# MLP loops written out, buffers released by the job count, a fifth block on TensorE, late sums moved

## The reference

```python
def first_block(x, c, w_ada, b_ada, w_in, ...):
    mod = jax.nn.silu(c) @ w_ada[l] + b_ada[l]
    shift1, scale1, gate1, shift2, scale2, gate2 = jnp.split(mod, 6, axis=-1)
    u = _layer_norm(x) * (1.0 + scale1[:, None, :]) + shift1[:, None, :]
    m = _token_mixer(u, w_in[l], ...)          # 4 retention heads, 4 GLA heads
    x = _layer_norm(DEEPNORM_ALPHA * x + gate1[:, None, :] * m, ln1_w[l], ln1_b[l])
    u2 = _layer_norm(x) * (1.0 + scale2[:, None, :]) + shift2[:, None, :]
    f = jnp.square(jax.nn.relu(u2 @ w_ff1[l])) @ w_ff2[l]
    x = _layer_norm(DEEPNORM_ALPHA * x + gate2[:, None, :] * f, ln2_w[l], ln2_b[l])

# retention, per head: chunk states by a recurrence
def step(R, U_i):
    return chunk_decay * R + U_i, R

def squared_relu_mlp(x, w1, w2):
    hdn = jnp.square(jax.nn.relu(jnp.einsum('bld,df->blf', x, w1)))
    return jnp.einsum('blf,fd->bld', hdn, w2)
```

## Time and profile before

| | us |
|---|---|
| median of 3 runs | 2861.61 |
| lowest, highest | 2859.59, 2868.67 |
| the profiled execution | 2858.77 |
| its span in the profile | 2857.0 |
| granted TensorE clock, mean over the span | 0.971 |
| TensorE busy | 2662.9 |
| VectorE, ScalarE, GpSimd busy | 1446.2, 948.0, 692.7 |

### The profile page before, as it was taken

The page is one execution under the profiler, slowest core; times in us unless marked ns, Lnnn a source line. Parts: engine busy times, 40 slices in busy tenths (PEclk is TensorE's granted clock), DMA queues, the critical chain, the costliest instruction groups (busy, mean ns, idle before and its releaser), DMA issues.

```text
span 2857.0 us, 34193 instructions
## 1 busy us (share of the span) xinstructions
PE 2662.9 (93%) x13332; PEld 1367.2 (48%) x13332; DVE 1446.2 (51%) x2304; ACT 948.0 (33%) x1120; POOL 692.7 (24%) x355
## 2 busy tenths in 40 slices
PE   7999989888999999999988899788999999999998
PEld 3677666433444444444464444344544444444443
DVE  6266444567444445576575749654336622222225
ACT  3323315025223322324254353253325232222231
POOL 1211123012212212311542231136113521221222
PEclk9999999998999999999989999999999999999999
DMA  7311131202111111221021230110011111110111
GB/s 303 115 53 60 49 119 38 95 30 89 36 54 59 44 44 59 74 89 45 31 89 59 74 116 29 45 59 30 29 34 42 59 59 31 59 60 30 59 45 59
DMA packets 55583, 182.34 MB, mean 64 GB/s; under 512 B 3952, under 2 KB 4368, under 8 KB 48016
## 3 DMA queue, kind: packets, MB, share of 16 engines
q1 hardware_dynamic: 47136, 138.89, 14.2%
q10 hardware_dynamic: 8304, 41.46, 4.0%
HBM read 170.90 MB, written 9.45 MB: 63 GB/s over the span
## 4 chain that ended last, share of the span: by engine, by line
PE 72%; DVE 10%; issue 4%; ACT 4%; DVEq 3%; POOLq 3%; PEld 1%; POOL 1%; DMA 1%; ACTq 0%; PEldq 0%; SPq 0%
PE PS L680 21%; PE PS L681 21%; PE PS L682 21%; POOLq L611 1%; POOLq L609 1%; DVE XT L2077 1%; PE PS L722 1%; PE PS L1425 1%; POOL WB L555 1%; PE PS L1398 1%; DVEq L2076 1%; ACT WS L1493 1%; PE PS L971 1%; ACT WB L1491 1%; DMA Hf<-in_w_ada 1%
## 5 line engine op out<-in xcount | busy, mean ns | idle before, releaser
L555 POOL TENSOR_TENSOR WB<-WS,WB 128x512 f16<-128x512 f32 (+1 forms) x264 | 495.1, 1907 | 1898.8 <-ACT WS L1493 1898.4
L680 PE MATMUL PS<-XT,WB 128*128 128x512 f16 x1568 | 599.1, 382 | 31.7 <-issue 15.5
L681 PE MATMUL PS<-XT,WB 128*128 128x512 f16 x1568 | 598.6, 382 | 0.0
L682 PE MATMUL PS<-XT,WB 128*128 128x512 f16 x1568 | 598.1, 381 | 0.0
L680 PE MATMUL PS<-WB,Hf 128*128 128x512 f16 x1440 | 550.8, 382 | 27.2 <-issue 6.9
L681 PE MATMUL PS<-WB,Hf 128*128 128x512 f16 x1440 | 550.2, 382 | 0.0
L682 PE MATMUL PS<-WB,Hf 128*128 128x512 f16 x1440 | 549.5, 382 | 0.0
L2075 DVE CAST Hf<-S 128x512 f16<-128x512 f32 x172 | 139.8, 813 | 497.7 <-ACT S L1735 411.1
L1491 ACT ACTIVATE WB<-WS 128x2048 f16<-128x2048 f32 (+3 forms) x118 | 212.4, 1800 | 513.7 <-PEq L689 476.8
L2435 DVE SCALAR_TENSOR_TENSOR R<-PS,R 128x512 f32<-128x512 f32 x208 | 143.0, 691 | 264.9 <-PE PS L682 257.9
L680 PEld LDWEIGHTS PS<-XT,WB 128*128 128x128 f16 x1568 | 154.3, 98 | 225.5 <-issue 29.5
(11 more groups left out here) (377 smaller groups left out, 2749.8 us busy)
## 6 DMA issues: line engine op xcount, KB each, us to landing
WS<-in_w_ff SPq DMA_DIRECT2D x32, 1024.0 KB, 5.1
WS<-in_mlp_w SPq DMA_DIRECT2D x32, 1024.0 KB, 5.1
WS<-in_w_mix SPq DMA_DIRECT2D x20, 1024.0 KB, 4.8
Hf<-in_w_ada ACTq DMA_DIRECT2D x12, 1024.0 KB, 6.0
Hf<-in_w_ada SPq DMA_DIRECT2D x8, 1024.0 KB, 10.5
WS<-in_w_out SPq DMA_DIRECT2D x8, 1024.0 KB, 5.1
R<-in_x SPq DMA_DIRECT2D x4, 1024.0 KB, 9.0
R<-in_x ACTq DMA_DIRECT2D x2, 2048.0 KB, 7.9
```

The lines of the kernel that those rows point to most:

```text
L555: op = pool.tensor_tensor(WB[:, slot, 1, at:at + n], WS[:, hf, i * n:(i + 1) * n], WB[:, slot, 0, at:at + n], ALU.subtract)
L680: pe.matmul(o, ah, bh, start=(first and k == 0), stop=False, skip_group_check=True)
L681: pe.matmul(o, ah, bl, start=False, stop=False, skip_group_check=True)
L682: mm = pe.matmul(o, al, bh, start=False, stop=(last and k == n - 1), skip_group_check=True)
```

## The change

Four edits.

1. `chunk_used` no longer drains TensorE. It notes, when the program is built, how many jobs have been issued; ScalarE waits for `job_done` to reach this number before it rounds into the slot. The two drains of this kind in the state-space stage go too. `reads_done` stays.
2. TensorE's loop in both MLPs becomes seven written-out pairs, with constants in the waits. The loops of the other engines stay.
3. Late block 5 is made by `late_job(5)` on TensorE; VectorE's `late_sum(5)` in head 3 is gone, and its evacuation takes the diagonal of the result (`mod_diagonal`).
4. In heads 0 to 2 `late_sum(h + 2)` stands ahead of the recurrence.

VectorE in head 1, before: from the evacuation of late block 2 (L2127) over the recurrence (L2281, L2284) and the late sum (L2183, L2186) to the head norm.

The register step and the branch are gone, the two waits at the first matmul of the next hidden chunk are the same. The diff, without the renumbered calls:

```diff
         @block.tensor
         def _(pe):
             J = [0]
             K = [0]
-            pe.sem_inc(w_used, 2)
-
-            def wide_bank(j=None, extra=0):
-
-                j = J[0] if j is None else j
-                if j >= 4 or not isinstance(extra, int):
-                    pe.wait_ge(evac[j % 4], j // 4 + extra)
+
+            def wide_bank():
+
+                j = J[0]
+                if j >= 4:
+                    pe.wait_ge(evac[j % 4], j // 4)
                 return j % 4
...
             def chunk_used():
-                pe.drain().then_inc(w_used, 1)
+                used_jobs.append(J[0])
...
                 if pr == 0:
-                    late_total(5)
+                    late_job(5)
...
-                with pe.Fori(0, 3) as i:
-                    pair(0, 4 * i, 12 * i)
-                    pair(1, 4 * i, 12 * i)
-                J[0] += 2 * 48
-                pair(6, 0, 0)
+                for u in range(NF - 1):
+                    pair(u)
...
-                pe.drain().then_inc(w_used, 2 - g)
+                used_jobs.extend([J[0]] * (2 - g))
...
             def round_half(slot, hf, n, loaded, used):
 
-                act.wait_ge(w_used, used)
+                if used is not None:
+                    act.wait_ge(job_done, used)
                 act.wait_ge(w_loaded[hf], loaded)
...
             def round_part(c, hf):
-                round_half(c % 2, hf, 4 * narrow.get(c, HALF), loaded_at[c], c + 1)
+                round_half(c % 2, hf, 4 * narrow.get(c, HALF), loaded_at[c], used_jobs[c - 2] if c > 1 else None)
...
-                        round_half(c % 2, hf, 2048, loaded_at[c] + 64 * i, c + 1 + 4 * i)
+                        round_half(c % 2, hf, 2048, loaded_at[c] + 64 * i, used_jobs[c - 2] + 48 * i)
...
-                elif i <= 5:
+                elif i <= 4:
                     mod_evac(4 + i)
                 else:
                     mod_diagonal(4 + i)
...
                 late_evac(h + 1)
+                if h < 3:
+                    late_sum(h + 2)
                 for g in range(2):
                     K[0] = ret_side(h, "u", g)
                     b = side_in()
...
                 dve.drain().then_inc(mix_v, 1)
-                late_sum(h + 2)
                 K[0] = ret_side(h, "o", 0)
```

More of the change, by code:

```diff
@@ L156, in program @@
         w_split = sem("w_split")
-        w_used = sem("w_used")
         job_done = sem("job_done")
@@ L452, in load_late @@
                 for hf in range(2):
-                    sp.wait_ge(*((late_used, 2) if i == 7 and hf == 0 else (job_done, LATE_JOBS[i - 1] + 1)))
+                    sp.wait_ge(*((late_used, 3) if i == 7 and hf == 0 else (job_done, LATE_JOBS[i - 1] + 1)))
                     sp.dma_start(LATE[hf].rearrange("p (j n) -> p j n", j=4),
@@ L650, in _ @@
                 pool.drain().then_inc(res_ready, 1)
+        used_jobs = []
         @block.tensor
@@ L1044, in mlp, with hidden_job @@
             def mlp(c0, src, last, rest_at):
-                def hidden_job(W, j, par, extra):
+                def hidden_job(W, j):
                     hf, f = j // 4, j % 4
-                    b = wide_bank(extra=extra)
+                    b = wide_bank()
                     gemm(PS[:, b, :], lambda k: hilo(W, k, f * P, (f + 1) * P),
@@ L1051, in hidden_job, with down_job @@
                     J[0] += 1
-                def down_job(W, j, par, extra):
+                def down_job(W, j, par):
                     t, n = j // 2, j % 2
-                    b = wide_bank(extra=extra)
+                    b = wide_bank()
                     gemm(PS[:, b, :], lambda k: (H[:, 0, 4 * par + k, t * P:(t + 1) * P],
@@ L1091, in mlp @@
                 for j in range(16):
-                    down_job(deep(c0 + 2 * NF - 1), j, 1, 0)
+                    down_job(deep(c0 + 2 * NF - 1), j, 1)
                     if j == 10 and not last:
@@ L2174, in late_evac, with late_sum @@
                     mod_diagonal(4 + i)
-            def late_sum(i):
-                for j in range(8):
+            def late_sum(i, halves=(0, 1)):
+                for j in range(4 * halves[0], 4 * halves[-1] + 4):
                     if j % 4 == 0:
@@ L2186, in late_sum @@
                         dve.scalar_tensor_tensor(LATE_SUM, w, f, LATE_SUM, ALU.mult, ALU.add)
-                dve.drain().then_inc(late_summed, 1)
+                if halves[-1]:
+                    dve.drain().then_inc(late_summed, 1)
             def columns_half(hf, dst):
```

14 lines of the change are left out of this document (7 added, 7 removed).

## The result

The changed kernel takes 2874.57 us (median of 20 runs, 2870.12 to 2876.65) against 2862.80 for the kernel before in the same comparison (20 runs, 2857.05 to 2871.08). The ratio is 1.0034, 95% interval 1.0026 to 1.0042: it is slower by 0.34%, and the measured median lies 1.6 us above the range of the prediction. The profiled execution of after took 2874.51 us with a span of 2872.7 and a mean granted clock of 0.967, against 2858.77, 2857.0 and 0.971 before: +15.7 us where the sum said -0.7.

The account below looks back on a forecast made before the run. TensorE, busy 93% of the span, was taken as the bound. Gains of 26.7 (MLPs) + 6.0 (other drains) less costs of 27.0 (late sums) + 5.0 (clock) gave -0.7 us; forecast 2861 us, range 2850 to 2873.

Parts of the forecast that it names:

- the sum: Whole kernel: gains 32.7 us less costs 32.0 us, net -0.7 us on the profiled execution's 2858.8 us.
- Price of a boundary: TensorE's chunk boundaries: 0.43 us each with a drain in written-out code, 0.5 to 0.65 in a loop, zero without drain.
- Back edges: TensorE's MLP loops: gaps of 0.75 us in the first, 3.93 and 4.34 in the second, with 1.6 us of clock each.
- Gain of the other drains: Drains outside the MLPs: 14 of 24 boundaries count at 0.43 us, gaining 6.0 us, bounds 2 and 10.
- Late sums: Retention heads 0 to 2: sums ahead of the recurrence wait for their load; TensorE stalls three times 9.0, 27.0 us.
- Clock on top: Output matmuls behind the three retention-head stalls run at lower clock: 3 x 1.65 = 5.0 us lost, bounds 0 and 9.
- Rival 2: Slower: clock recovers late after the three head stalls, 2.9 us each, and outside drains give only 2; 2869 us; chance 0.22.
- Fifth block: Late block 5 on TensorE: 3.6 us of matmuls replace 1.0, hidden ahead of an 8.86 us wait; costs nothing.
- rival 1: Slower: waits left at 41 chunk boundaries cost what the drain's gap did, 17.6 us less gain, 2878 us; chance 0.08.
- 3 (rotation waits that go): Retention heads: VectorE, free earlier, finishes the rotation before TensorE asks, removing 3.21 us waits and 1.6 us clock; 2856; chance 0.15.
- 4 (no stall): Retention heads, faster: block there in time or sum ends before TensorE asks; 32 us remain, 2829 us; chance 0.04.
- the 310.03 row: Matmul at 310.03 waits for a weight split and a bank without a drain right ahead; no idle time beside it.

## Why the prediction was wrong

**Price of a boundary: right.** The gaps went, and in the MLPs the sum held: -19.3 us against 18.0 in the second, -6.7 in the first against 8.6. In the second MLP the gain is of three parts: with drains and the loop held 11.8 us, with drains and written out 14.1, without drains 19.3.

**Back edges: right in size, wrong in kind.** I priced 3.93 and 4.34 us as what a back edge of the second MLP costs, and said of the 0.75 us in the first only that the rows stand. The difference between the two loops, equal in their bodies, should have been asked after: the second is fetched again, the first is held. The written-out code shows no such gap in the changed kernel, so the forecast for the change came true.

**Gain of the other drains: this step failed.** It gave them +6.0 us "bounds 2 and 10". What they did in the traces was nothing in most places and -7.0 in the state-space stage: a term of the sum with the wrong sign. There were two errors. The bounds did not go below zero, although a drain also holds TensorE back: where TensorE then waits for a slower engine, it arrives earlier without it and waits longer, and half clock behind the longer wait is a loss on top. And the clock was looked up behind the waits that the change adds, not behind those that it lengthens: from 1.10 us to 1.68, and from 1.51 to 3.13, with half clock behind. The runs with the six and with the four drains put back show that it was these drains (-5.5 and -5.3 us in that stretch). That the clock has its part in the loss is read from the traces; why the waits together grew by more than the drains gave stays open. In the heads the rotation waits took what the drains gave, as forecast: 0.74, 3.66 and 0.70 us against 0.30, 3.21 and 0.24. In attention and S5, +0.2.

**Late sums: right.** 27.0 us forecast, 26.5 in three waits, each between 8.6 and 9.1; that the load sets it and not the sum is shown by the run with the earlier load. **Clock on top: a little short.** The output matmuls of a head took 5.4, 5.7 and 5.9 us where they took 3.35, 6.9 us more in all against 5.0. Rival 2 put 2.9 on this and 2 us on the outside drains; it came out nearest (2869), and for the reason that it named in part.

**Fifth block: right, by luck.** I took 16 matmuls of 7.10 us for two late jobs and halved them. They are one: eight fp32 matmuls show as 16 records, as the four small ones show as eight. `late_job(5)` alone shows as

```profile
391.06 7.03 PE L723 MATMUL PS<-Hf,SM 128*128 128x512 f32 x16
400.99 1.46 PE L930 MATMUL PS<-BASE,R 128*128 128x128 f32 x8 [2.90 <-DVEq L2338]
```

The job costs 7.0 us, twice the forecast, and the wait ahead of the scaled keys, 8.86 before, is down to 2.90. It was hidden with 2.9 us to spare. That the edit moves the second loop's code in the kernel before, and costs 6.6 us there, has no bearing on the forecast: in the changed kernel there is no such loop.

**The other rivals.** Nothing of rival 1 (a boundary that stays), 3 (rotation waits that go) or 4 (no stall) was found; the 310.03 row was a fair witness for boundaries without a drain.

**The sum.** The profiled execution of before was 4.0 us under the median of its 20 runs, that of after at its own median: of the 16.4 us between forecast and trace the medians show 12.5. The table sets one execution against one, and the one of before is a quick one. The kernel with the sums in front has its numbers in the later stretches, but in three other kernels that keep these drains (loops written out, fifth block alone, all drains back) the state-space stretch took 311.2 to 311.5 us and the one behind it 305.5 to 305.7, against 309.68 and 303.79, and the first 486.9 to 491.0 against 485.72. Beside those three the loss in the state-space stretch is 5.2 to 5.5 us, and the other stretches gain a little. Taking the MLPs (-26.0) and the stalls with their clock (26.5 + 6.9) from the traces, the medians' +11.8 leave a loss of 4.4 us for the outside drains and all else, where a gain of 6.0 was forecast. The step that failed is the same, its size lies between 4 and 7 us of loss.

## What to carry to other kernels

A drain or another short hold of the busiest engine is not only a cost: ahead of a wait it can be absorbed, and without it the same wait is longer and may be followed by half clock, so price its removal stage by stage and let the bounds go below zero. An operation moved ahead of another brings its loads with it, so look where they land before the order is changed. If a loop on TensorE has idle time at its back edges in one place and not in another, look at the instruction packets in the trace: here it was the loop's place in the code, which an edit ahead of it moved.

## What the runs showed of the hardware

- A loop of some 1560 instructions on TensorE was held or fetched again at each pass by where it lies: 9 instruction packets of some 16 KB, or 26 to 27; at a back edge 0.7 us, or 3.9 to 7.1 us (with drains), nothing, or 2.0 to 2.3 us (without). A shift of 12 instructions (36 or 48 drains as padding) decided. TensorE's first loop, as long, had 8 packets from 730 to 1290 us in each of the kernels with loops.
- Behind a wait of 1.10 us in the state-space stage the granted clock stayed at 1.00 (1602.8 to 1610.2, before). Behind one of 1.51 us the first eight matmuls ran at full clock and the next ones did not; from 1572.8 to 1583.1 the mean is 0.83:

```profile
1572.80:1583.10 10.30, 10.08 (x40) 5.14 (x40) 8.38 (x19) 0.76 (x2) 0.00 (x0) 0.83 0.22 90
```

  Behind 3.13 us the same work was slow from its first matmul (1.97 us for the eight), and the mean is 0.72 over 11.2 us:

```profile
1603.60:1614.80 11.20, 11.14 (x40) 6.68 (x41) 8.42 (x20) 0.60 (x1) 0.00 (x0) 0.72 0.20 83
```

- 36 drains in a row cost nothing that shows where TensorE waited 3.7 us anyway.
- The late job's eight fp32 matmuls of 512 columns show as 16 records and take 7.0 us; records are no count of operations there.
